# Splitting each gate/up matmul of a mixture-of-experts layer into four by groups of 32 output partitions

## What is computed

```
def expert_block(args):                       # 128 slots of one expert
    tok, g, e = args
    xb = t_pad[tok]                           # 128 x 1024
    hid = jax.nn.silu(xb @ w_gate[e]) * (xb @ w_up[e])      # 128 x 256
    return (hid @ w_down[e]) * g[:, None].astype(xb.dtype)  # 128 x 1024
...
routed = jax.ops.segment_sum(yb.reshape(n_slots, d), tok_buf, num_segments=n_tok + 1)[:n_tok]
shared = (jax.nn.silu(t @ ws_gate) * (t @ ws_up)) @ ws_down
```

## Time and profile before

| | |
|---|---|
| median of 2 runs | 1528.79 us (1527.85 to 1529.73) |
| span of the profiled execution | 1532.3 us |
| TensorE busy | 1311.5 us (86%), 4370 MATMUL records |
| DVE, ACT, POOL busy | 468.8, 248.5, 196.0 us |
| expert stage | from 690.5 us on, some 740 us |
| TensorE's mean granted clock | 0.918 of 2.4 GHz |
| HBM | 216 GB/s over the span |

### The profile page before, as it was taken

The page is one execution under the profiler, slowest core; times in us unless marked ns, Lnnn a source line. Parts: engine busy times, 40 slices in busy tenths (PEclk is TensorE's granted clock), DMA queues, the critical chain, the costliest instruction groups (busy, mean ns, idle before and its releaser), DMA issues.

```text
span 1532.3 us, 12587 instructions
## 1 busy us (share of the span) xinstructions
PE 1311.5 (86%) x4370; PEld 696.2 (45%) x4370; DVE 468.8 (31%) x959; ACT 248.5 (16%) x526; POOL 196.0 (13%) x274
## 2 busy tenths in 40 slices
PE   6999556699999798969999999999999999999100
PEld 3446543475444544624454554544544544544000
DVE  2764545421010211651122122121221221221188
ACT  3302124421010302101111111111111111111010
POOL 2000033000000000021212212212112122121000
PEclk9999775699999899889999999999999999999655
DMA  5231140024163003303888888888888878884560
GB/s 163 81 101 17 18 117 0 1 85 163 55 239 145 28 28 104 141 12 125 333 332 317 341 334 322 326 315 326 329 315 318 329 295 329 324 313 182 202 297 28
DMA packets 80073, 299.92 MB, mean 196 GB/s; under 512 B 26197, under 2 KB 28442, under 8 KB 54938
## 3 DMA queue, kind: packets, MB, share of 16 engines
q1 hardware_dynamic: 61594, 264.68, 46.2%
q0 software_dynamic: 18432, 34.64, 5.9%
HBM read 292.97 MB, written 37.88 MB: 216 GB/s over the span
## 4 chain that ended last, share of the span: by engine, by line
PE 60%; issue 29%; DVE 7%; DMA 2%; ACT 2%; POOL 0%; SPq 0%; POOLq 0%; DVEq 0%
PE ps L868 29%; PE ps L858 14%; PE ps L551 7%; DVE z L1683 4%; PE ps L874 4%; PE ps L885 1%; DMA ring<-expert_rows 1%; PE ps L611 1%; PE ps L680 1%; DVE z L1443 1%; DMA h<-in_x 1%; PE ps L666 1%; DVE st L1431 1%; PE ps L668 1%; PE ps L667 1%
## 5 line engine op out<-in xcount | busy, mean ns | idle before, releaser
L868 PE MATMUL ps<-ring,z 128*128 128x512 f32 x1024 | 453.0, 595 | 1.1 <-DVE z L1639 1.1
L868 PEld LDWEIGHTS ps<-ring,z 128*128 128x128 f32 x1024 | 191.1, 192 | 217.7 <-issue 217.7
L551 PE MATMUL ps<-dw,act_t 128*128 128x512 f32 x576 | 251.3, 598 | 4.5 <-issue 3.6
L858 PE MATMUL ps<-ring,tok 128*128 128x512 f32 x512 | 230.4, 593 | 0.9 <-DVE tok L1654 0.9
L551 PEld LDWEIGHTS ps<-dw,act_t 128*128 128x128 f32 x576 | 110.2, 192 | 142.3 <-issue 141.2
L1647 DVE SCALAR_TENSOR_TENSOR tok<-tok,gcb,ps 128x256 f32<-128x256 f32 x64 | 30.7, 480 | 416.2 <-ACT tok L1128 409.8
L858 PEld LDWEIGHTS ps<-ring,tok 128*128 128x128 f32 x512 | 92.6, 191 | 93.4 <-issue 92.3
L1634 DVE COPY z<-ps 128x512 f32<-128x512 f32 x64 | 44.3, 692 | 176.8 <-PE ps L858 176.8
L1128 ACT ACTIVATE tok<-ps 128x256 f32<-128x256 f32 x64 | 24.6, 384 | 416.9 <-PE ps L868 416.9
L1723 POOL COPY ixb<-tabs 128x1 uint32 (+1 forms) x128 | 24.3, 190 | 483.7 <-DVE z L1634 483.3
L1744 POOL DMA_INDIRECT expert_rows<-z,ixb x64 | 65.2, 1018 | 55.5 <-POOL ixb L1723 52.1
(11 more groups left out here) (265 smaller groups left out, 1078.3 us busy)
## 6 DMA issues: line engine op xcount, KB each, us to landing
ring<-in_w_gate SPq DMA_DIRECT2D x64, 1024.0 KB, 4.8
ring<-in_w_up SPq DMA_DIRECT2D x64, 1024.0 KB, 7.5
ring<-in_w_down SPq DMA_DIRECT2D x64, 1024.0 KB, 10.7
ring<-expert_rows SPq DMA_DIRECT2D x4, 4096.0 KB, 18.6
dw<-in_w_in SPq DMA_DIRECT2D x8, 1024.0 KB, 5.4
dw<-in_wk_x SPq DMA_DIRECT2D x4, 1024.0 KB, 6.5
dw<-in_wv_x SPq DMA_DIRECT2D x4, 1024.0 KB, 4.9
dw<-in_w_out SPq DMA_DIRECT2D x4, 1024.0 KB, 4.9
```

Of the source, the lines that this page charges most:

```text
L551: ins = pe.matmul(ps[0:m, bank0 + j, 0:n], lhs(w, q * 4 + c4, c4, j), rhs(w, q * 4 + c4, c4, j), start=(q == 0 and c4 == 0), stop=(q == le ...
L858: ins = pe.matmul(ps[:, 5 + n, :], htt[j % 2][:, c, :], ring_wd(j)[:, c, n * 512:(n + 1) * 512], start=(c == 0), stop=(c == 1))
L868: ins = pe.matmul(ps[:, 2 + j % 2, :], xtt[j % 2][:, c, :], ring_wgu(j)[:, :, c, :], start=(c == 0), stop=(c == NC_D - 1))
```

## The change

Each gate/up matmul becomes four. Each takes 32 of the 128 columns of the same stationary slice (32 slots), the whole moving operand as before, and writes to the 32 partitions of the same bank that belong to these slots. The four of a slice c follow each other, and each group of partitions adds up its own eight slices. Semaphores and everything on other engines are as they were; the last matmul still tells of the end.

```
--- before.py
+++ after.py
@@ -865,8 +865,10 @@
             pe.wait_ge(e_xta, e + 1)
             pe.wait_ge(e_xtv, e + 1)
             for c in range(NC_D):
-                ins = pe.matmul(ps[:, 2 + j % 2, :], xtt[j % 2][:, c, :], ring_wgu(j)[:, :, c, :],
-                                start=(c == 0), stop=(c == NC_D - 1))
+                for q in range(4):
+                    rows = slice(q * 32, (q + 1) * 32)
+                    ins = pe.matmul(ps[rows, 2 + j % 2, :], xtt[j % 2][:, c, rows], ring_wgu(j)[:, :, c, :],
+                                    start=(c == 0), stop=(c == NC_D - 1))
             ins.then_inc(e_gu, 1)
             if not last:
                 pe.wait_ge(xg_ld[(j + 1) % 4], it * 16 + 16 * (1 + (j + 1) // 4))
```

## The result

The kernel with the split takes 1550.42 us (1549.24 to 1551.60, 2 runs) against 1528.79 us before: 21.6 us or 1.4% more by the medians. The ratio that goes with the interval is an estimate from the same runs and not the quotient of the medians: 1.0119, 95% interval 1.0088 to 1.0150. In a later job, beside some of the experiments, it took 1554.0 us against 1531.9 us, 22.1 us more, ratio 1.0129 (1.0108 to 1.0150). The loss is 1.2 to 1.4%, inside the 2% line.

A forecast was written before the change was run, and what follows sets the result against it. TensorE was taken to bound the 64 experts. Steps in and out, 0.265 us per expert or 17.0 us, plus 3 us for the slots made +20 us on 1528.8: 1549 us, range 1535 to 1575.

The forecast's parts named there:

- The slot of four: Gate/up: four passes to different partition groups run together in one pass's time; 1024 slots add 3 us (0 to 7.5).
- my estimate of 12 us: Gate/up slots by the Trainium skill: each further tile adds about 4 ns, 1024 x 3 x 4 ns, where the forecast had 3.
- Loads and issue: Gate/up: four loads of 32 columns for one of 128 stay hidden under the passes, and issue keeps up; nought.
- In: Step from the whole-array hidden turns into split gate/up, once per expert: 0.12 us lost (0.10 to 0.14).
- Out: Step from split gate/up to the whole-array token turns, once per expert: 0.145 us lost (0.14 to 0.15).
- A: Rival, gate/up: only two groups run together, each slot becomes two, +439 us, 1985 us with the steps; 6%.
- B: Rival, gate/up: the four passes run one after another, +1318 us, 2864 us; 4%.
- C: Rival, gate/up: each slot 10 to 25 ns longer, 1556 to 1572 us; 9% up to 1575, 2% beyond.
- E: Rival, expert loop: steps in and out cost nothing because next loads are done ahead, 1529 to 1535 us; 4%.
- D: Rival, expert loop: code no longer stays in the engine, 14 rounds each wait for a block, 1563 to 1591 us; 4%.
- Clock: TensorE in the expert stretch: granted clock stays at 1.00, the 2.4 GHz level.
- The DMA share: DMA engines' busy share in the expert stretch: falls from 0.80 to 0.78.

The follow-up runs named there:

- plain turns: The split kernel with token turns reading 128 adjacent channels, not every eighth one: 1546.5 us, ratio 1.0087 to the kernel before.
- the last experiment: The split kernel with gate/up for 64 slots only, slices 0 to 3 and 4 to 7 side by side: 1444.6 us, ratio 0.942 to the kernel before.

## Why the prediction was right

*The bound.* The chain is TensorE's before and after, and each microsecond per expert counted 64 times.

*The slot of four.* Foretold as one pass's time from a pair (L645) and found so: 0.429 us. The term was +3 us (0 to 7.5); L868's 453.0 us busy became 455.5, of which the longer first slot is 64 x 0.02; the starts leave nothing for the slots themselves: 0. Per further group the starts lie 7 ns apart (0.02 us for three), and the Trainium skill (TensorE: Matmul & The Clock Gate, "Part 3: Packing small matmuls") has 4 ns for it. The mistake would be to charge it to each slot, as my estimate of 12 us by that page of the Trainium skill did: each group keeps its distance, and it is paid once, at the end of the row of passes.

*Loads and issue.* Nought was right: L870's loads are 127.6 us busy under the passes.

*In.* 0.12 us foretold; 0.117 by the starts (medians of 62 experts in the trace: 0.210 for 0.117 to the first slot, and 0.453 for 0.429 to the second).

*Out.* 0.145 us foretold, 0.216 measured: 0.11 to the load, and 0.10 for the load itself. This is the mis-sized term, by 4.5 us in all: 0.05 of the 0.07 us is the load, 0.02 that four passes start one behind the other. My rows for it, L655 and L626, were turns that load from neighbouring columns, with loads 0.14 us long; the strided turns behind L870 have loads 0.19 long, and with nothing to hide under the first of them shows, 0.10 us of it for 0.05. The plain turns took this 0.05 back. I had also said that L876 would take as long as before; the bare load lies in its 1.09 us. The rows to take for the load were those of the same instruction, L874 itself.

*The sum.* 64 x 0.333 = 21.3 us for 17.0, and 0 for 3: the total of 20 is near the measured 21.6 because the two errors have opposite signs.

*Rivals.* A, B and C fall with the slot of 0.429 us, E with the step in. A was nearer than it looks: with the loops in the other order it costs 1000 us. What made four groups run was that they stood next to each other in the program, and my prediction gave no thought to order. D: one block of code moved in 14 rounds, and not one in each. That agrees with the room for 2048 instructions that Runtime: NRT & Kernel Launch ("Instruction fetch mechanics") of the Trainium skill gives.

*The rest.* Clock as foretold. The DMA share seems to contradict me, 0.81 for 0.80 from 705 to 1420 us, but that window ends behind the last weight transfers, whose last issue comes 14 us later after the change (1402.7 us for 1388.5). Where they run in both kernels, from 750 to 1380 us, the share falls by the two points foretold and the rate by the 3% by which an expert is longer. Windows of before, then of after:

```profile
750.00:1380.00 630.00, 630.00 (x1876) 1.00 0.84 323
```

```profile
750.00:1380.00 630.00, 630.00 (x4392) 1.00 0.82 313
```

## What to carry to other kernels

A matmul split by groups of output partitions streams at no extra cost, but each change between whole-array and split matmuls costs 0.09 us in which nothing starts, and a first load that nothing hides, 0.12 us in and 0.2 us out here: split long rows of matmuls and never single ones. Put matmuls of different groups next to each other, at most two f32 matmuls (four passes) per group before the next group's turn. The split pays only if the groups do different work, such as two experts with at most 64 tokens side by side: gate/up fell to half in the last experiment, until the weight transfers were the bound. Such a kernel was not built here.

## What the runs showed of the hardware

TensorE does not start all its passes in the order of the program: with partition groups, a pass overtakes up to three waiting ones of each other group (52 slots for 64 passes; 36 with blocks of four slices, 16 with blocks of two). The Trainium skill has matmuls of all tiles in program order (TensorE: Matmul & The Clock Gate, "Part 3: Packing small matmuls"); here the measurement decides otherwise for the starts. The Trainium skill's rule that changing the tiling mode drains the engine (TensorEngine Tiling (Array Packing), "Key Properties") agrees with the traces: some 0.1 us from the possible start of the next pass to its load, after a pass of 32 moving columns as after one of 512.
